# A mixer and expert block: the expert loop's order on TensorE, its form switch and its 32-wide products changed, with several stages ahead of the output projection

## What is computed

```python
top_val, top_idx = lax.top_k(logits, TOP_K)          # TOP_K = 4 of 32
...
def expert_block(args):                              # a block of up to 128 token slots of one expert
    xblk, e = args
    gate = xblk @ w_gate[e] + b_gate[e]
    up = xblk @ w_up[e] + b_up[e]
    gate = jnp.minimum(gate, SWIGLU_LIMIT)
    up = jnp.clip(up, -SWIGLU_LIMIT, SWIGLU_LIMIT)
    h = (up + 1.0) * gate * jax.nn.sigmoid(SWIGLU_ALPHA * gate)
    return h @ w_down[e] + b_down[e]
...
y = segment_sum(yb * row_w[:, None], row_tok)        # each token adds its four weighted rows
```

## Time and profile before

| | |
|---|---|
| median of 3 runs | 2683.56 us (2679.57 to 2684.94) |
| the profiled execution | 2680.95 us, span of its instructions 2679.1 us |
| mean granted TensorE clock | 0.963 of full speed |
| busy: TensorE products | 2422.3 us, 90% |
| busy: DVE, ACT, POOL | 921.2, 486.7, 413.7 us |
| chain that ended last, by engine | PE 84%, DVE 9%, issue 3% |
| read from memory, written | 548.47 MB, 38.27 MB |

### The profile page before, as it was taken

How to read it: one execution, slowest core, us unless ns; L and a number is a source line. 1 busy time by engine, 2 the same in 40 slices (tenths; PEclk the granted TensorE clock), 3 DMA queues, 4 the chain that set the end, 5 groups by cost and what they waited for, 6 DMA issues and landing times.

```text
span 2679.1 us, 35693 instructions
## 1 busy us (share of the span) xinstructions
PE 2422.3 (90%) x11737; PEld 1214.5 (45%) x11784; DVE 921.2 (34%) x1880; ACT 486.7 (18%) x1097; POOL 413.7 (15%) x376
## 2 busy tenths in 40 slices
PE   5999999977884899999999999999999999999992
PEld 3575766663452444444443334433444444434430
DVE  3144536571465222313322233222333323222224
ACT  4121222222441110101110111111111111010111
POOL 5000000004000112111112122122221212212122
PEclk9999999999986899999999999999999999999996
DMA  9112120205022768595899979979877898989875
GB/s 329 32 40 79 40 79 16 87 29 209 32 114 82 253 226 272 157 307 180 269 362 315 321 241 342 356 262 352 260 257 266 292 355 275 332 310 303 310 256 176
DMA packets 213755, 587.60 MB, mean 219 GB/s; under 512 B 20010, under 2 KB 79778, under 8 KB 213698
## 3 DMA queue, kind: packets, MB, share of 16 engines
q1 hardware_dynamic: 131698, 338.21, 34.7%
q10 hardware_dynamic: 53200, 193.02, 20.3%
q0 software_dynamic: 28800, 55.59, 9.8%
HBM read 548.47 MB, written 38.27 MB: 219 GB/s over the span
## 4 chain that ended last, share of the span: by engine, by line
PE 84%; DVE 9%; issue 3%; ACT 1%; POOL 1%; DMA 1%; DVEq 0%; ACTq 0%; SPq 0%; POOLq 0%
PE ps L1582 24%; PE ps L1608 14%; PE ps L1640 12%; PE ps L1658 7%; PE ps L1362 4%; PE ps L1466 4%; PE ps L1358 3%; PE ps L1365 2%; PE ps L1422 2%; PE ps L1551 2%; PE ps L1368 1%; PE ps L1618 1%; PE ps L1334 1%; PE ps L1540 1%; PE ps L1600 1%
## 5 line engine op out<-in xcount | busy, mean ns | idle before, releaser
L1582 PE MATMUL ps<-w_gate_e,xT 128*128 128x512 f32 x736 | 345.8, 592 | 0.0
L1582 PE MATMUL ps<-w_up_e,xT 128*128 128x512 f32 x736 | 345.8, 592 | 0.0
L1640 PE MATMUL ps<-w_down_e,hT 128*128 128x512 f32 x736 | 319.6, 592 | 0.0
L1216 DVE TENSOR_SCALAR oh_gu<-part_e,tab_e 128x128 bf16<-128x128 f32 x48 | 13.9, 290 | 852.1 <-PE ps L1582 543.3
L571 POOL DMA_INDIRECT xg<-xn_rows,gidx x49 | 51.0, 1041 | 1553.5 <-DVE sidx_tab L1207 1490.5
L797 ACT ACTIVATE sig_sb<-gate_sb 128x1024 f32<-128x1024 f32 x47 | 49.7, 1057 | 1160.0 <-DVE gate_sb L1222 1140.5
L1608 PE MATMUL ps<-w_gate_e,xT 128*32 128x256 f32 (+1 forms) x1504 | 236.1, 486 | 0.0
L1608 PE MATMUL ps<-w_up_e,xT 128*32 128x256 f32 (+1 forms) x1504 | 229.9, 474 | 0.0
L1582 PEld LDWEIGHTS ps<-w_up_e,xT 128*128 128x128 f32 x736 | 139.8, 190 | 176.0 <-issue 176.0
L1640 PEld LDWEIGHTS ps<-w_down_e,hT 128*128 128x128 f32 x736 | 139.8, 190 | 168.3 <-issue 165.0
L1582 PEld LDWEIGHTS ps<-w_gate_e,xT 128*128 128x128 f32 x736 | 139.8, 190 | 168.3 <-issue 165.0
(11 more groups left out here) (308 smaller groups left out, 2591.5 us busy)
## 6 DMA issues: line engine op xcount, KB each, us to landing
w_down_e<-in_w_down_dram ACTq DMA_DIRECT2D x368, 512.0 KB, 4.6
w_gate_e<-in_w_gate_dram SPq DMA_DIRECT2D x256, 512.0 KB, 5.6
w_up_e<-in_w_up_dram SPq DMA_DIRECT2D x256, 512.0 KB, 6.8
w_ring<-in_w_ada_dram SPq DMA_DIRECT2D x17, 1024.0 KB, 5.4
w_ring<-in_w_in_dram SPq DMA_DIRECT2D x20, 512.0 KB, 5.1
w_first<-in_w_ada_dram SPq DMA_DIRECT2D x7, 1024.0 KB, 12.5
y_rows<-box POOLq DMA_DIRECT2D x10, 512.0 KB
x_all<-in_x_dram SPq DMA_DIRECT2D x2, 2048.0 KB, 10.7
```

The costliest lines, as they stand in the source:

```text
L1582: last = T.matmul(ps[:, b, :], xT[:, k, :], wgt[b // 2][:, k, (b % 2) * 512:(b % 2) * 512 + 512], start=False, stop=k == KT - 1)
L1640: last = T.matmul(ps[:, 4 + b, :], hT[:, k, :], wgt[2][:, k, b * 512:b * 512 + 512], start=False, stop=k == KT - 1)
```

## The change

In the expert loop: the register loads of expert and form, and the branch, are moved ahead of `hidden`, which is now repeated inside each branch of `gate_up`; `slot_sums` goes ahead of `down`; DVE clamps `up` before `gate` and counts a new `up_evac` after it, for which `slot_sums` waits; the sigmoid now waits for the second of the two; form 2 (and the half and the quarter by themselves) goes through k four at a time, the half's and then the quarter's. One pass less is in the loop, so that more of the program stands ahead of it and behind it. Ahead of the output projection: ACT takes the first part's eight transposed groups and DVE the second's; two ada pieces come after part 0 and three after part 1 instead of one and two; heads 0 to 3 have 3, 2, 2 and 9 of the 16 ada pieces, seven of them set one by one between head 3's "v" units; the ring of weights gets its buffers accordingly; the box means of groups 2 and 3 both go to head 1 and all are cut into three parts, one after each state batch; the zeros are sent after `mod` is there; `slot_ids` gets a place of its own and is written after the last level instead of after the last unit.

```diff
@@ units
+        def values_and_ada(h, count):
+            vals, home = len(chunks), ring_home()
+            chunk([(w_in, 3 * HG + h * P, P), (w_in, 4 * HG + h * P, P)], [], home)
+            for t in range(NT):
+                units.append(("v", h, t, vals))
+                if t >= NT - count:
+                    n = rest_ada.pop(0)
+                    chunk([(w_ada, n * QW, QW)], [("a", n)], (home + 1 + len(chunks) % 2) % 3)
...
-            values(h)
-            by_levels.append(len(units))
             if h == 3:
+                values_home = values_and_ada(h, 7)
+                by_levels.append(len(units))
+                last_ada(values_home)
                 mixed(h - 1)
-            more_ada(1)
...
+                more_ada((3, 2, 2)[h])
...
+        BOXES = ((0, 1), (2, 3), (), ())
+        X_ACT = [*range(KT), *range(2 * KT, 3 * KT, 2)]
+        X_DVE = [*range(KT, 2 * KT), *range(2 * KT + 1, 3 * KT, 2)]
+        X_UNITS = (range(0, 2), range(2, 5), range(5, n_ada_first))
@@ POOL
             pool.wait_ge(zeros_set, 1)
+            pool.wait_ge(mod_ready, 1)
...
-            pool.wait_ge(proj_psum, len(units))
+            pool.wait_ge(lev_put, 2 * HEADS * LEVELS)
             link(G.memset(slot_ids[:], 0.5))
@@ ACT
             def sigmoid(m):
-                act.wait_ge(gate_ready, m + 1)
+                act.wait_ge(gu_evac, m + 1)
@@ DVE, state batches
+                box_parts = iter(())
+                for g in BOXES[h]:
+                    box_parts = itertools.chain(box_parts, box_means(g))
                 for j, (d, lo, hi) in enumerate(BATCHES):
...
-                for g in ((0, 1), (2,), (3,), ())[h]:
-                    box_means(g)
+                    next(box_parts, None)
@@ DVE, expert items
+                V.tensor_scalar(up_sb[:], ps[:, 2:4, :].rearrange("p a n -> p (a n)"), SWIGLU_LIMIT, -SWIGLU_LIMIT,
+                                ALU.min, ALU.max).then_inc(up_evac, 1)
                 V.tensor_scalar(gate_sb[:], ps[:, 0:2, :].rearrange("p a n -> p (a n)"), SWIGLU_LIMIT, None, ALU.min
-                                ).then_inc(gate_ready, 1)
-                V.tensor_scalar(up_sb[:], ...).then_inc(gu_evac, 1)
+                                ).then_inc(gu_evac, 1)
...
             slots(0, link, first=True)
+            one_hot(oh_gu, 0).then_inc(oh_ready, 1)
             build_sel(1, link)
             slots(1, link)
             build_sel(2, link)
-            one_hot(oh_gu, 0).then_inc(oh_ready, 1)
@@ TensorE
             def slot_sums(m):
                 pe.wait_ge(sel_ready, m + 1)
                 if not (isinstance(m, int) and m < 2):
-                    pe.wait_ge(gu_evac, m - 1)
+                    pe.wait_ge(up_evac, m - 1)
...
             def gate_up(m):
                 e = item_expert(pe, m)
+                v = item_variant(pe, m)
+                with pe.If(v == 3):
+                    hidden_and_free(m)
+                    whole_gate_up(m, e)
+                for some, parts in enumerate(PARTS):
+                    with pe.If(v == some):
+                        hidden_and_free(m)
+                        small_gate_up(m, e, parts)
+
+            def hidden_and_free(m):
+                if not (isinstance(m, int) and m < 1):
+                    hidden(m - 1)
                 pe.wait_ge(xT_ready, m + 1)
...
-                for k in range(KT):
-                    pe.wait_ge(gu_in[k], e * 32 + 32)
-                    for lo, N, bank in parts:
-                        C = N * D // P
+                for k0, (lo, N, bank) in itertools.product((0, KT // 2), parts):
+                    C = N * D // P
+                    for k in range(k0, k0 + KT // 2):
+                        if bank == parts[0][2]:
+                            pe.wait_ge(gu_in[k], e * 32 + 32)
...
-            hidden(0)
-            with pe.Fori(0, n_last) as i:
-                gate_up(i + 1)
+            gate_up(1)
+            n_before = item_before_last(pe)
+            with pe.Fori(0, n_before) as i:
                 rows(i + 2)
+                slot_sums(i + 3)
                 down(i)
-                slot_sums(i + 3)
-                hidden(i + 1)
+                gate_up(i + 2)
+            rows(n_last + 1)
+            slot_sums(n_last + 2)
+            down(n_before)
+            hidden(n_last)
             down(n_last)
```

More of the change, by code:

```diff
@@ L188, in ring_home, with chunk_before @@
             return (len(chunks) - KT + 1) % 3
+        def chunk_before(n):
+            return max(m for m in range(n) if homes[m] == homes[n])
         def free_units(new_units):
@@ L209, in queries, with last_ada @@
             chunk([(w_in, h * P, P)], [("q", h, 0, part) for part in range(2)], ring_home())
+        def values_and_ada(h, count):
[6 more added lines that the diff above has]
+                    chunk([(w_ada, n * QW, QW)], [("a", n)], (home + 1 + len(chunks) % 2) % 3)
+            chunks[vals] = (chunks[vals][0], len(units))
+            return home
+        def last_ada(home):
+            while rest_ada:
+                n = rest_ada.pop(0)
+                chunk([(w_ada, n * QW, QW)], [("a", n)], (home + 1 + len(chunks) % 2) % 3)
         def values(h):
@@ L691, in turned @@
             def turned(part):
-                for g in range(part * KT, (part + 1) * KT, 2):
+                for g in X_ACT:
+                    if g // KT != part:
+                        continue
                     k, t0, nt, _ = XGROUPS[g]
@@ L876, in turned @@
             def turned(part):
-                for g in range(part * KT + 1, (part + 1) * KT, 2):
+                for g in X_DVE:
+                    if g // KT != part:
+                        continue
                     k, t0, nt, _ = XGROUPS[g]
@@ L898, in _ @@
             dve.wait_ge(mod_ready, 1)
[L899 removed]
+            dve.wait_ge(xt0_act, len(X_ACT))
+            dve.wait_ge(xt0_dve, len(X_DVE))
             for g in range(1, len(XGROUPS), 2):
@@ L1387, in turn @@
                     last.then_inc(xt0_psum, 1)
-            turn(0)
-            run(range(0, 1))
-            turn(1)
-            run(range(1, 3))
-            turn(2)
-            run(range(3, n_ada_first))
+            for part in range(len(XPARTS)):
+                turn(part)
+                run(X_UNITS[part])
             ada_columns()
@@ L1562, in gate_up @@
                 apart(pe)
-                v = item_variant(pe, m)
-                with pe.If(v == 3):
-                    whole_gate_up(m, e)
-                for some, parts in enumerate(PARTS):
-                    with pe.If(v == some):
-                        small_gate_up(m, e, parts)
             def whole_gate_up(m, e):
@@ L1609, in small_gate_up @@
                                                 wgt[w][:, k, j * C:(j + 1) * C], start=False, stop=k == KT - 1)
-                    last.then_inc(gu_used, 1)
+                        if bank == parts[-1][2]:
+                            last.then_inc(gu_used, 1)
             def hidden(m):
@@ L1651, in small_down @@
                                  start=True, stop=False)
-                for k in range(KT):
-                    pe.wait_ge(dn_in[k], m * 16 + 16)
-                    for _, N, bank in parts:
-                        C = N * D // P
+                for k0, (_, N, bank) in itertools.product((0, KT // 2), parts):
+                    C = N * D // P
+                    for k in range(k0, k0 + KT // 2):
+                        if bank == parts[0][2]:
+                            pe.wait_ge(dn_in[k], m * 16 + 16)
                         at, kk = divmod(k, KT * N // P)
@@ L1660, in small_down @@
                                             wgt[2][:, k, j * C:(j + 1) * C], start=False, stop=k == KT - 1)
-                    last.then_inc(d_used, 1)
+                        if bank == parts[-1][2]:
+                            last.then_inc(d_used, 1)
             pe.wait_ge(tables, 1)
```

53 lines of the change are left out of this document (30 added, 23 removed).

## The result

The changed kernel takes 2730.49 us (median of 4 runs, 2726.88 to 2734.33) where the kernel before takes 2683.77 (2679.57 to 2684.94): ratio 1.0177, 95% interval 1.016 to 1.0194, so 46.7 us slower. The profiled execution took 2730.77 us with a span of 2728.7, which is 49.8 us more than the profiled execution of before.

The account below looks back on a forecast made before the run. TensorE was taken as the bound; -51 + 23 + 131 - 33 + 25 - 39 + 7 = +63 us on 2680.95 gave 2744, or 2747 us for the runs' median. Own range 2700 to 2795, whole range 2635 to 2815 us.

Parts of the forecast that it names:

- Part 1: Expert loop, form chosen ahead of `hidden`: the gap before the gate's bias products goes, -51 us; loads before `hidden` cost +23.
- Part 2: Expert loop, slot sums ahead of `down`: 1.65 us idle before the sums and 1.2 behind, each pass, +131 us.
- Part 3: Form 2's gate and down products, four k at a time: fewer changes between half and quarter widths, -33 us.
- Part 4: TensorE's clock in the expert loop: falls behind idle stretches in about 13 passes, +25 us.
- Part 5: Stages ahead of the output projection: POOL chain, box means, ada pieces and start together gain, -39 us.
- Part 6: Both ends of the expert loop: more program runs for the first time, +7 us.
- (B): Rival, expert loop: register load runs under the sums' wait, no clock falls; -82 us, 2602 us, chance 0.17.
- (C): Rival, expert loop: wait real, sequencer quick, 1.2 us ahead of the sums, 0.6 behind; -24, 2660 us, chance 0.16.
- (D): Rival, expert loop: clock falls in nearly every pass, +86 us in place of +25; 2808 us, chance 0.12.
- (E): Rival, early stages: they give little as landings move along, up to +30 us, 2777; chance 0.55 together with own case.

Follow-up runs that it names:

- e2: Changed kernel with the slot sums back behind the down products, form still chosen ahead of `hidden`: 2596.7 us, 0.9689 of the kernel before.
- e11: e10 with the branch on the form back behind `hidden`: 2584.4 us, 0.9641 of the kernel before.
- e3: Changed kernel with all four register loads of a pass made at its top, waits and branches left in place: 2644.4 us, 0.9864 of the kernel before.
- e4: Changed kernel with DVE's gate clamp ahead of the up clamp again, sums still waiting for up: 2829.4 us, 1.0556 of the kernel before.
- e7: Changed kernel with the slot sums' register load made twice behind their wait: 2788.0 us, 1.0385 of the kernel before.
- e6: Kernel before with the early stages and with form 2 and the small forms four k at a time: 2609.0 us, 0.9728 of the kernel before.
- e1: Kernel before with only the changed stages ahead of the output projection: 2643.2 us, 0.9851 of the kernel before.
- e5: Changed kernel with twelve unused identity transposes between the row transposes and the slot sums' wait: 2703.9 us, 1.0075 of the kernel before.
- e12: Kernel before with only `slot_ids` in its own place, written after the last level: 2668.0 us, 0.9954 of the kernel before.
- e9: e10 with the slot sums ahead of the down products, as in the changed kernel: 2632.6 us, 0.9816 of the kernel before.
- e8: Changed kernel with sums behind `down` and one load of four values at the top of the pass: 2586.1 us, 0.9636 of the kernel before.
- e10: Changed kernel with sums behind `down` and one load of four values behind the row transposes: 2581.3 us, 0.9623 of the kernel before.

## Why the prediction came out as it did

The sign and the place were right: 2730 us measured, 2747 said, slower because of the slot sums ahead of `down`. Step by step, measured in the account above:

**Part 1, the form ahead of `hidden`.** -51 said, 53.4 to 3.5 us measured, -50, and e2 and e11 show that it was the loads and the branch that stood there. The gap into `hidden` was said to be +23; it is 6.7 + 3.1, so +10: none behind forms 1 and 3, 1.1 us on average behind form 0, 0.68 behind form 2. I put 0.5 us on the average pass, and it is 0.2, since a whole or half down leaves enough in the queue. This is the largest over-estimate of the sum.

**Part 2, the sums ahead of `down`.** +131 said, 87 + 42 = +129 measured. The total is right by two errors that cancel. Ahead of the sums 76 was said and 87 came: behind the clamp stand 1.29 to 1.44 us, not the 0.96 of the one place in the earlier trace rows. That place is not the same sequence, though the prediction says so: its load has a constant index, and it has 0.98 us in the changed kernel too. I had also said that the view would name DVE's up clamp as the releaser; it has "issue", and only the chain shows the clamp. Behind the sums 55 was said and 42 came. The form steps are there: without a second set, the gap ahead of `down` is 1.03 us for form 1 and 1.30 for form 2 (said: 0.26 a step). e2 shows that the step as a whole is what makes the kernel slower, e3, e4 and e7 that its mechanism is the one given: a wait that ends with the up clamp, and a load that does not begin until then. On this point the Trainium skill (Perfetto Trace Analysis, Per-engine timelines), by which a sequencer-only instruction holds the sequencer in its wait, agrees with e3 and e7 (1.0 us less, 0.68 more).

**Part 3, four k at a time.** -33 said. In the trace form 2's gate products are 21.26 us (said: 21.1), the downs 1.7 shorter at full clock, 29 us in all; e6 against e1 gives 33, within a few us.

**Part 4, the clock.** +25 said. The downs of forms 3, 1 and 2 lose about 35 us to it (17.5, 7.5 and 10), the gates of form 2 that fell before win 6: +29. The size came out by luck: 22 downs lost 1.6 us each, where I had said about 13 passes at 2.3. e5 shows the cause and gives 27 back.

**Part 5, the early stages.** -39 said, -34.9 in the trace at `slot_sums(0)`, and e1 has 36 to 40. Its pieces were sized less well. The start gave 5.6 (6 said). Box means and ada gave 10.2 (20 said): the wait of 16.3 us is gone and that for `att` fell from 14.7 to 4.2, but 10.7 us now stand at the states (L1490 and L1500; 3.7 before), 3.2 at `diag_t` (L1399) and 3.6 at the ada weights (L1383), so more than the 2 us that I gave back. The POOL chain gave the rest, 18.5 at L1521, where 13 was said "not more, because the landing sets it". The landing does set it, but it moved: the bias rows are issued 16 us sooner in the changed kernel and land at 610.73. e12 has the issues where they were and moves the chain by 10 and not 13: the last rows land at 633.56, since I had taken the median of 7.9 us from issue to landing, and the slowest of the nine takes 11.

**Part 6, both ends of the loop.** +7 said. What is left of the account is about -4: `gate_up(0)` stands idle for 2.2 instead of 5.7 us, and what stands for the first time elsewhere is small.

Sum: -50 + 10 + 129 - 29 + 29 - 35 - 4 = +50, the 49.8 measured. Of the rivals, (B) is ruled out by e3 and e7, (C) by the 1.94 us ahead of the sums (1.2 said), (D) by the 11 of the loop's 22 whole downs that ran at full clock (13.90 us), (E) by e1. One figure of the forecast does not fit its own sum: by these terms 2700 to 2795 us is a loss of 1.2 to 3.3 us net a pass, not 1.4 to 3.0.

## What to carry to other kernels

A table value that a sequencer reads costs nothing under a full queue and its whole price behind a wait that has yet to be met, so what is loaded, not only what is waited for, decides where a step can stand. Before a block is moved ahead of another, look at what it waits for in its new place and at what is loaded behind that wait. An idle stretch between short blocks can be paid twice, once as idle and once in the clock of the products behind it (e4, e5); e9 paid only the first.

The parts can be had without the price: e8 and e10 keep the early stages, the four k and the form ahead of `hidden`, leave the sums behind `down`, and run in 0.9636 and 0.9623 of the time before.

## What the runs showed of the hardware that I had not expected

- One more microsecond of idle ahead of the sums in each pass cost 99 us where 55.7 us of idle came in (e4): clock 0.957 to 0.935. And 1.5 us of work that nobody needs, put in an idle stretch, made the kernel 26.6 us faster (e5).
- In the loop a first register load behind a wait costs 1.0 us and one right behind it 0.68; with a constant index both cost 0.66 to 0.68 (`slot_sums(0)`, changed kernel and e7).
- One load of four values is cheaper than four single ones, but not free: at the top of the pass it stands 0.8 us bare behind form 2's gate, where the four stand 2.0 (e8, e3), and moved behind eight transposes of 1.04 us it was still bare by as much in all (e10).
- The sums without a second set start some 0.13 us later than those with one (0.42 and 0.29 us in e3). It looks as if the branch were cheaper when its body is run; no run tests that.
